# Streaming encoder layer on one core: the gate of p by seven half products a pair, and the end by halves of the tokens

## Chip, core and metric

One core of one Trainium2 chip runs the kernel. The metric is the device time of one execution in microseconds (us), less being better. Three executions of the kernel before took 1573.99, 1574.2 and 1575.36 us; the median is 1574.2.

## What is computed

One layer of a hybrid encoder on 1024 prompt frames and 32 new frames, in fp32, D_MODEL = 1024. The part that matters here is the second half of the layer and its end:

```python
x = x + merged @ w_out
ffn_out, new_conv = conv_ffn(rmsnorm(x, g_ffn), conv_buf, w_up, w_dw, b_dw, w_down)
x = x + ffn_out
x = x + (p_i @ w_ple) * jax.nn.sigmoid(rmsnorm(x, g_ple) @ w_ple_gate)
...
y_prompt = rmsnorm(xp, g_final)
```

conv_ffn multiplies by w_up (1024 x 5632), convolves one half of the result over three frames, applies GELU, multiplies by the other half, and multiplies by w_down (2816 x 1024). Ahead of it lie an RMS norm, an input projection, pooling, banded attention of 8 heads and two gated projections.

## The kernel before

The tokens lie along the columns: T = 1056 = 1024 + 32, in three chunks of CW = 352 or in two halves of HT = 528. The channels lie on the 128 partitions, in KT = 8 tiles. Every fp32 product is made of three matmuls on a high and a low part of each factor (high x high, high x low, low x high). ACT rounds to the high part, DVE (for tokens) and POOL (for weights) subtract it to get the low part. The five engines run side by side; each instruction list is written out by hand and runs in order, and semaphores join them.

Weights come from w_stream. SP loads them in order; in the feed-forward a frame's tiles come in four halves (half_raw(0) to half_raw(3), 128 x 512). A load waits with half_free until POOL has made the low part of the piece that lay there. POOL's and ACT's pieces go through a ring of four places: piece q waits until PE is done with piece q - 4 (piece_event). pieces_upto on ACT makes the high parts up to a count, ahead of need.

The feed-forward is a list of frames. An up frame U (n = 0 to 21) makes two tiles of w_up, one of each half, with seven products of half size in the place of eight (Strassen's way in Winograd's form): seven weight pieces, of which some are sums of halves, against seven token operands op_hi/op_lo 0 to 6, each of HK = 4 tiles of HT columns. A frame has 7 x 4 x 3 x 2 = 168 matmuls of 264 columns (L952). A down group D (0 to 10) adds two rows of tiles to the residual x_res: UNITS = 24 units (8 tiles x 3 chunks), each of 6 matmuls of 352 columns (L976 to L978), in 8 banks; DVE adds each unit to x_res (down_add, L1829). The order is U0 U1 U2 D0 U3 U4 D1 ... U20 U21 D9 D10.

Behind D10 stands the end. p's product (K = 256, product(), L703) fills ple; the norm of x is summed on PE (norm, L741), rooted on ACT, inverted on DVE (invert_rms). The gate of p is eight tiles of 8 x 9 = 72 matmuls of 352 columns (L703), each read by DVE (scaled), passed through the sigmoid on ACT, multiplied by ple and added to x_res. Then the last norm, one reciprocal of 1056 columns, eight products by g_final (L1940) and eight stores. p itself is loaded by SP into p_raw, which shares its place with operands 5 and 6, so it has to wait until the last up frame's products are done:

```python
sp.wait_ge(ffn_done, UP[FT - 1].event + PRODUCTS)
sp.dma_start(p_raw[:], pT).then_inc(p_loaded, 16)
sp.wait_ge(piece_split, PIECES)
```

This stands behind the loop over all frames. At the start of the feed-forward the five operands 0 to 4 are made while w_out's product runs; operands 5 and 6 and the three sums of the norm (norm2, L960) come between the first frame's products, and root2 and invert2 make the reciprocals by thirds.

## Time and profile before

| what | us |
|---|---|
| median of three executions | 1574.2 |
| the profiled execution's own time | 1574.24 |
| its span | 1572.5 |
| busy: PE, DVE, POOL, ACT | 1517.8, 852.7, 676.3, 496.5 |
| mean granted TensorE clock | 0.989 of full speed |

The span runs from the first to the last instruction on the core; the rest of the execution's time lies around it. Engine names: PE is TensorE, DVE VectorE, ACT ScalarE, POOL GpSimd, SP SyncE, which here only issues DMAs. Matmuls overlap in the pipeline, so a matmul's own length is longer than its pitch, and the pitch is what counts. A granted clock of 1.00 is 2.4 GHz and 0.50 is 1.2 GHz. "Idle before" names what released an engine.

### The profile page before, as it was taken

Reading aid. Unit: us, or ns where it says so; the run is one execution under the profiler, and the core shown is the slowest. Engines: PE = TensorE matmul, PEld = TensorE weight load, DVE = VectorE, ACT = ScalarE, POOL = GpSimd, SP = SyncE. Lnnn points to the kernel's source line nnn. Section 1 sums busy time; section 2 is a strip of 40 time slices with the busy share of each in tenths; the row PEclk is TensorE's granted clock in tenths of the full one; section 3 lists DMA queues with packets and bytes.
Section 4 is the critical chain, followed back from the end, with each engine's and each line's share of the span. In section 5 each row is a group of like instructions: output and inputs, shape, how many; then the busy total and the mean of one; then the engine's idle time right before and its main releaser. Section 6 shows DMA issues by size and latency. Waiting matters only on the chain.

```text
span 1572.5 us, 25547 instructions
## 1 busy us (share of the span) xinstructions
PE 1517.8 (97%) x10616; PEld 1474.2 (94%) x10616; DVE 852.7 (54%) x1305; ACT 496.5 (32%) x875; POOL 676.3 (43%) x436
## 2 busy tenths in 40 slices
PE   7999999999999999998999999999999999999992
PEld 7988888889999999998999999999999999999992
DVE  7564444442231136668746547456474574687665
ACT  6025444443100021244432423323233233432211
POOL 2431213223343434345664655746556466623330
PEclk9999999999999999999999999999999999999996
DMA  6410212100111114111111201112012110311102
GB/s 239 138 43 15 71 58 69 35 27 28 41 54 41 41 54 151 41 33 49 55 37 52 74 28 54 55 43 66 28 55 63 46 55 28 99 52 41 41 14 110
DMA packets 37402, 91.33 MB, mean 58 GB/s; under 512 B 5528, under 2 KB 5536, under 8 KB 37160
## 3 DMA queue, kind: packets, MB, share of 16 engines
q1 hardware_dynamic: 34552, 80.95, 15.8%
q10 hardware_dynamic: 2736, 8.76, 1.4%
q8 instruction: 84, 1.38, 0.4%
q14 instruction: 30, 0.25, 0.0%
HBM read 83.00 MB, written 9.83 MB: 59 GB/s over the span
## 4 chain that ended last, share of the span: by engine, by line
PE 89%; DVE 5%; issue 2%; DMA 1%; ACT 1%; SPq 0%; POOL 0%; DVEq 0%; ACTq 0%; POOLq 0%
PE ps L703 28%; PE ps L952 27%; PE ps L976 5%; PE ps L978 5%; PE ps L977 5%; PE ps L715 4%; PE ps L717 4%; PE ps L716 4%; PE ps L838 2%; PE ps L860 2%; PE ps L812 2%; DVE h_lo L1369 1%; DMA x_in<-xT 1%; DVE acc L1429 1%; DVE x_res L1940 1%
## 5 line engine op out<-in xcount | busy, mean ns | idle before, releaser
L623 POOL TENSOR_TENSOR w_hi<-w_raw,zero 128x1024 fp32r<-128x1024 f32 x56 | 106.0, 1892 | 542.5 <-PE ps L703 252.2
L657 POOL TENSOR_TENSOR w_lo<-w_raw,w_hi 128x512 fp32r<-128x512 f32 x154 | 221.5, 1445 | 215.2 <-ACT w_hi L1198 215.2
L952 PE MATMUL ps<-op_hi,w_hi 128*128 128x264 f32 x1232 | 252.9, 286 | 3.7 <-DVE op_lo L1696 2.2
L952 PE MATMUL ps<-op_lo,w_hi 128*128 128x264 f32 x1232 | 252.2, 286 | 0.0
L952 PE MATMUL ps<-op_hi,w_lo 128*128 128x264 f32 x1232 | 251.8, 286 | 0.0
L952 PEld LDWEIGHTS ps<-op_hi,w_hi 128*128 128x128 f32 x1232 | 193.1, 189 | 5.3 <-DVE op_lo L1696 2.4
L952 PEld LDWEIGHTS ps<-op_lo,w_hi 128*128 128x128 f32 x1232 | 192.1, 189 | 0.0
L952 PEld LDWEIGHTS ps<-op_hi,w_lo 128*128 128x128 f32 x1232 | 191.8, 189 | 0.0
L715 PE MATMUL ps<-h_hi,w_hi 128*128 128x352 f32 x480 | 160.9, 335 | 10.5 <-DVE w_lo L1411 8.9
L976 PE MATMUL ps<-mid_hi,w_hi 128*128 128x352 f32 x528 | 170.2, 322 | 0.0
L977 PE MATMUL ps<-mid_lo,w_hi 128*128 128x352 f32 x528 | 170.0, 322 | 0.0
L978 PE MATMUL ps<-mid_hi,w_lo 128*128 128x352 f32 x528 | 170.0, 322 | 0.0
L1829 DVE TENSOR_TENSOR x_res<-ps,x_res 128x352 f32<-128x352 f32 x264 | 130.0, 520 | 52.0 <-PE ps L978 52.0
L717 PE MATMUL ps<-h_hi,w_lo 128*128 128x352 f32 x480 | 156.0, 325 | 0.0
L716 PE MATMUL ps<-h_lo,w_hi 128*128 128x352 f32 x480 | 155.7, 324 | 0.0
L1198 ACT ACTIVATE w_hi<-w_raw 128x512 fp32r<-128x512 f32 x154 | 97.2, 632 | 182.1 <-PE ps L952 98.6
L625 POOL TENSOR_TENSOR w_lo<-w_raw,w_hi 128x1024 fp32r<-128x1024 f32 x56 | 148.5, 2652 | 4.4
L703 PE MATMUL ps<-h_hi,w_hi 128*128 128x352 f32 x480 | 104.3, 325 | 3.7 <-DVE gap L1383 1.5
L703 PE MATMUL ps<-h_hi,w_lo 128*128 128x352 f32 x480 | 103.4, 323 | 0.0
L703 PE MATMUL ps<-h_lo,w_hi 128*128 128x352 f32 x480 | 103.3, 323 | 0.0
L715 PEld LDWEIGHTS ps<-h_hi,w_hi 128*128 128x128 f32 x480 | 91.7, 191 | 11.6 <-issue 8.9
L978 PEld LDWEIGHTS ps<-mid_hi,w_lo 128*128 128x128 f32 x528 | 99.4, 188 | 0.0
(207 smaller groups left out, 2768.6 us busy)
## 6 DMA issues: line engine op xcount, KB each, us to landing
w_raw<-w_stream SPq DMA_DIRECT2D x132, 256.0 KB, 2.8
w_raw<-w_stream SPq DMA_DIRECT2D x58, 512.0 KB, 3.7
x_in<-xT SPq DMA_DIRECT2D x8, 528.0 KB, 8.6
x_res<-xT ACTq DMA_DIRECT2D x8, 528.0 KB, 6.8
o_y<-x_res ACTq DMA_DIRECT2D x8, 528.0 KB, 2.9
bias_lines<-bias_line SPq DMA_DIRECT2D x1, 3072.0 KB
bias_sb<-bias_lines SPq DMA_DIRECT2D x4, 640.0 KB, 5.8
o_v<-vT SPq DMA_DIRECT2D x4, 272.0 KB, 2.1
```

The source lines that it names most:

```text
L623: pool.tensor_tensor(w_hi[k][:], w_raw[k][:], zero[:].broadcast_to([P, KT * P]), ALU.add).then_inc(w_hi_done, 1)
L625: pool.tensor_tensor(w_lo[k][:], w_raw[k][:], w_hi[k][:].bitcast(F32), ALU.subtract).then_inc(w_split, 1)
L657: pool.tensor_tensor(piece_lo(q), x, piece_hi(q).bitcast(F32), ALU.subtract).then_inc(piece_split, 1)
L703: mm = pe.matmul(out[:, c, :], w, x[:, c * CW:(c + 1) * CW], start=first and n == 0, stop=last and n == 2)
L715: pe.matmul(out, w_hi[k][:, col], x_h, start=b == 0, stop=False)
L716: pe.matmul(out, w_hi[k][:, col], x_l, start=False, stop=False)
L717: mm = pe.matmul(out, w_lo[k][:, col], x_h, start=False, stop=b == KT - 1)
L952: mm = pe.matmul(region(fr, i, c), w[:, col], x[i][:, b, c * HW:(c + 1) * HW], start=opens and b == 0 and n == 0, stop=b == HK - 1 and n == 2,
L976: pe.matmul(out, piece_hi(q)[:, col], x_h, start=b == 0, stop=False)
L977: pe.matmul(out, piece_hi(q)[:, col], x_l, start=False, stop=False)
L978: mm = pe.matmul(out, piece_lo(q)[:, col], x_h, start=False, stop=b == 1)
L1829: dve.tensor_tensor(x, bank(fr.unit_bank(u), CW), x, ALU.add).then_inc(ffn_read, 1)
```

## The change

1. **Gate of p by half products.** Four frames H (n = 22 to 25) are put behind the feed-forward, two tiles of w_ple_gate each, with the same seven products as an up frame, in another order (ROLES, OPERANDS, PIECE_HALF). The operands 0 to 6 are now made of x after the feed-forward, scaled by g_ple. Four quarters of a pair (two tiles, two halves of the tokens: quarter) are read, scaled by the reciprocals, passed through the sigmoid, multiplied and added by turns. The copies out of the first three products go to tmp and a spare half row.
2. **Last down group and p's product as one frame Z.** MIXED lists the 24 units of D10 and behind them 24 units of p's product, in the same eight banks. DVE adds two units at once (down_pair, 704 columns). ACT copies p's units two at once to ple (ple_out). Between these, DVE (first_ops, second_ops), ACT (tile_ops) and POOL (base_out, x times g into p_raw's place) make operands 0 to 4 as each tile is finished, and the sum of squares.
3. **p is loaded behind the loads of U21**, ahead of those of D9, since Z and H need loads of their own.
4. **End by halves of the tokens.** The last norm is summed, rooted, inverted and multiplied for the right half and then for the left; 16 stores of 264 KB go from SP and ACT by turns.
5. **Roots ahead at the start of the feed-forward.** The third sum of the norm goes behind product 5 of the first frame; on ACT the first two roots stand ahead of the high parts of operand 6, the third behind them.

The core of the diff:

```diff
+FREES = {"U": (2, 0, 1, 3), "H": (1, 0, 2, 3), "D": (2, 0, 1, 3), "Z": (2, 0, 1, 3)}
-FRAMES += [("U", FT - 2), ("U", FT - 1), ("D", GROUPS - 2), ("D", GROUPS - 1)]
+FRAMES += [("U", FT - 2), ("U", FT - 1), ("D", GROUPS - 2), ("Z", GROUPS - 1)]
+FRAMES += [("H", FT + _r) for _r in range(KT // 2)]
+MIXED = [("D", _u) for _u in range(UNITS)] + [("E", _u) for _u in range(UNITS)]
...
@@ sync: loads @@
+                if fr is UP[FT - 1]:
+                    sp.wait_ge(ffn_done, fr.event + PRODUCTS)
+                    sp.dma_start(p_raw[:], pT).then_inc(p_loaded, 16)
+            for i in range(0, 2 * KT, 2):
+                sp.wait_ge(y_ready, i + 1)
+                cols = slice(HT, T) if i < KT else slice(0, HT)
+                sp.dma_start(o_y[i % KT][:, cols], x_res[:, i % KT, cols]).then_inc(stored, 16)
...
@@ gpsimd @@
+            def base_out(i):
+                pool.wait_ge(ffn_read, tile_read(i))
+                pool.wait_ge(p_split, 2)
+                pool.tensor_tensor(base_row(i), x_res[:, i, 0:HT],
+                                   g_sb[:, 2 * KT + i:2 * KT + i + 1].broadcast_to([P, HT]), ALU.mult).then_inc(y_made, 1)
+                    for i in range(fr.pieces):
+                        if i in (4, 6):
+                            base_out(i - 4)
+                            base_out(i - 3)
+                        piece_low(fr.piece + i, half_raw(HALVES[i % 4]))
...
@@ tensor @@
+            def mixed():
+                for s, (kind, u) in enumerate(MIXED):
+                    if s % 6 == 0:
+                        pe.wait_ge(piece_split, q + 1)
+                    if s < 8:
+                        pe.wait_ge(ffn_read, fr.read + s - 7)
+                    elif MIXED[s - 8][0] == "D":
+                        pe.wait_ge(ffn_read, fr.read + MIXED[s - 8][1] // 2 + 1)
+                    else:
+                        pe.wait_ge(ple_read, MIXED[s - 8][1] // 2 + 1)
...
             up(0, 4, ready=(5, 5))
-            pe.wait_ge(root_done, 4)
-            norm2(2, bank(0, CW))
             up(0, 5, ready=(21, 1))
+            pe.wait_ge(root_done, CH + 1)
+            norm(2, 2, bank(0, CW))
             up(0, 6, ready=(25, 1))
...
@@ scalar @@
+            def tile_ops(m):
+                act.wait_ge(ffn_read, tile_read(m))
+                i = m % HK
+                if m < HK:
+                    op_high(0, i, x_res[:, m, 0:HT], m, 0, gain=2)
+                    square(x_res[:, m, :], 2 * KT + m)
+                    op_high(1, i, None, None, 20 + i + 1)
+                else:
+                    op_high(3, i, x_res[:, m, 0:HT], m, 0, gain=2)
+                    op_high(2, i, None, None, 24 + 2 * i + 1)
+                    square(x_res[:, m, :], 2 * KT + m)
+                    op_high(4, i, None, None, 24 + 2 * i + 2)
...
+            def copy_h(r, name, i):
+                act.wait_ge(ffn_done, fr.event + i + 1)
+                if r > 0:
+                    act.wait_ge(h_added, 4 * (r - 1) + 2 + i)
...
@@ vector @@
+            def down_pair(r):
+                dve.wait_ge(ffn_done, LAST.event + MIXED.index(("D", 2 * r)) + 2)
+                dve.tensor_tensor(x, out, x, ALU.add).then_inc(ffn_read, 1)
...
+            dve.wait_ge(h_added, 2 * KT)
+            for n, half in ((1, slice(HT, T)), (2, slice(0, HT))):
+                invert(3 * CH + n, half)
+                dve.wait_ge(rms_ready, 3 * CH + n)
+                for k in range(KT):
+                    dve.scalar_tensor_tensor(out=x_res[:, k, half], in0=x_res[:, k, half], scalar=g_col(3, k),
+                                             in1=rms[:, half], op0=ALU.mult, op1=ALU.mult).then_inc(y_ready, 1)
```

First listing: SP's list around the load of p, before. The 128x512 loads are halves of down tiles, the last of them those of D10.

```order
L606 DMA w_raw0_49<-w_stream 128x512 [waits piece_split]
L606 DMA w_raw1_50<-w_stream 128x512 [waits piece_split]
L608 DMA p_raw_113<-pT 128x2112 [waits ffn_done]
L540 DMA w_raw1_50<-w_stream 128x1024 [waits w_split,piece_split]
L540 DMA w_raw0_49<-w_stream 128x1024 [waits w_split]
```

And now; the two halves ahead of p are the last of U21, the two behind it the first of D9.

```order
L641 DMA w_raw0_50<-w_stream 128x512 [waits piece_split]
L641 DMA w_raw1_51<-w_stream 128x512 [waits piece_split]
L660 DMA p_raw_113<-pT 128x2112 [waits ffn_done]
L641 DMA w_raw0_50<-w_stream 128x512 [waits piece_split]
L641 DMA w_raw1_51<-w_stream 128x512 [waits piece_split]
```

The load of p, with its wait for U21's last product, moved from behind D10's four loads to ahead of D9's; 28 loads of halves now follow it.

Second listing: DVE's list at the last down group, before. x_res<-ps is the add of a unit, h_lo the low part of a tile of the gate's input.

```order
L1820 TENSOR_TENSOR mid_lo_108<-b_row_110,mid_hi_104 128x1056 [waits mid_hi_done,mid_ready]
L1829 TENSOR_TENSOR x_res<-ps,x_res 128x352 [waits ffn_done] x12
L1864 TENSOR_TENSOR p_lo<-p_raw,p_hi 128x1056 [waits p_hi_done] x2
L1829 TENSOR_TENSOR x_res<-ps,x_res 128x352 [waits ffn_done] x10
L1369 SCALAR_TENSOR_TENSOR h_lo<-x_res,g_sb,h_hi 128x1056 [waits hi_done,ffn_read]
```

And now, around the twelfth and last pair of the group (the x_res row near the end):

```order
L2033 TENSOR_TENSOR x_res<-ps,x_res 128x704 [waits ffn_done] x2
L1592 TENSOR_TENSOR acc<-acc,tmp 128x1056 [waits acc_done,sq_done]
L1883 SCALAR_TENSOR_TENSOR op_sum_88<-x_res,g_sb,op_sum_85 128x528 [waits ffn_read]
L1881 TENSOR_TENSOR op_sum_94<-op_sum_88,p_raw 128x528 [waits op_sum]
L1891 TENSOR_TENSOR op_lo_84<-op_sum_85,op_hi_83 128x528 [waits op_hi_done]
L1893 SCALAR_TENSOR_TENSOR op_lo_90<-x_res,g_sb,op_hi_89 128x528 [waits op_hi_done]
L1891 TENSOR_TENSOR op_lo_87<-op_sum_88,op_hi_86 128x528 [waits op_hi_done,op_sum]
L1891 TENSOR_TENSOR op_lo_93<-op_sum_94,op_hi_92 128x528 [waits op_hi_done]
L2033 TENSOR_TENSOR x_res<-ps,x_res 128x704 [waits ffn_done]
```

A sum of squares and six operand instructions stand ahead of the last read of the group's banks.

Third listing: ACT's list where p's first two units are copied out of their banks (ple<-ps). The four rows ahead of it are tile 5's; tile 4's four stand ahead of these. Before, DVE read p's product and ACT had only the high parts and squares here.

```order
L1297 ACTIVATE op_hi_89<-x_res,g_sb 128x528 [waits ffn_read]
L1295 ACTIVATE op_hi_86<-op_sum_88 128x528 [waits op_sum]
L1128 ACTIVATE tmp<-x_res 128x1056 [waits acc_done]
L1295 ACTIVATE op_hi_92<-op_sum_94 128x528 [waits op_sum]
L1438 ACTIVATE ple<-ps 128x704 [waits ffn_done]
L1288 ACTIVATE w_hi_52<-w_raw_51 128x512 [waits ffn_done,half_loaded3]
```

Each of the four waits for DVE, and the copy that frees two banks of PE comes behind them.

## Rows read from the trace of the kernel before

**Rows 1.** Page, part 4: shares of the chain by engine.

```profile
PE 89%; DVE 5%; issue 2%; DMA 1%; ACT 1%; SPq 0%; POOL 0%; DVEq 0%; ACTq 0%; POOLq 0%
```

**Rows 2.** Windows of PE by stage: window, length, busy (instructions), granted clock, DMA share, GB/s.

```profile
1393.10:1416.30 23.20, 23.03 (x144) 1.00 0.22 70
1416.30:1441.70 25.40, 23.85 (x144) 1.00 0.12 42
1441.70:1458.10 16.40, 13.62 (x78) 1.00 0.11 33
1458.10:1539.90 81.80, 81.77 (x504) 1.00 0.08 27
1539.90:1572.50 32.60, 3.49 (x6) 0.61 0.33 133
```

**Rows 3.** Chain of waits, last up frames: start, length, what.

```profile
1339.95 29.98 PE ps L952 x245
```

**Rows 4.** Timeline of PE, start of the feed-forward; in brackets idle time before.

```profile
717.96 1.54 PE L960 MATMUL ps<-acc,ones 128*128 128x352 f32 x2 [3.78 <-ACT rms L1261]
...
727.45 0.64 PE L952 MATMUL ps<-op_hi,w_hi 128*128 128x264 f32 x2 [2.17 <-DVE op_lo L1696]
...
736.18 0.48 PE L952 MATMUL ps<-op_hi,w_hi 128*128 128x264 f32 x2 [0.33 <-ACT b_row L1238]
```

**Rows 5.** Windows of PE: granted clock behind two idle stretches.

```profile
718.00:721.00 3.00, 3.00 (x11) 0.53 0.00 0
...
1545.00:1548.00 3.00, 0.66 (x1) 0.50 0.00 0
```

**Rows 6.** Timelines of DVE and ACT, second up frame.

```profile
732.83 1.22 DVE L1784 TENSOR_TENSOR a_row<-a_row,rms 128x1024 f32<-128x1024 f32 x1
...
735.45 0.59 ACT L1238 ACTIVATE b_row<-ps 128x528 f32<-128x528 f32 x1
```

**Rows 7.** DMA issues, w_raw's tile view, SP's timeline.

```profile
w_raw<-w_stream SPq DMA_DIRECT2D x132, 256.0 KB, 2.8
...
p_raw<-pT SPq DMA_DIRECT2D x1, 1056.0 KB, 6.8
...
L606 SPq DMA_DIRECT2D w_raw<-w_stream x16: 327/328/328, 1310.4 to 1372.1; - x16
...
1372.46 0.43 SPq L608 DMA_DIRECT2D p_raw<-pT  x1
```

**Rows 8.** Groups by line of ACT, 690 to 745 us.

```profile
L1205 ACT ACTIVATE op_hi<-op_sum 128x528 fp32r<-128x528 f32 x6 | 3.8, 642 | 10.9 <-DVE op_sum L1686 10.9
...
L1261 ACT ACT_TABLE_LOAD x1 | 1.3, 1283 | 0.0
...
L1238 ACT ACTIVATE b_row<-ps 128x528 f32<-128x528 f32 x2 | 1.2, 592 | 0.0
```

**Rows 9.** Timelines of DVE and POOL, last up frames and groups.

```profile
1348.99 1.80 DVE L1789 TENSOR_TENSOR b_row<-b_row,rms 128x528 f32<-128x528 f32 x1
...
1370.20 0.70 DVE L1789 TENSOR_TENSOR b_row<-b_row,rms 128x528 f32<-128x528 f32 x1
...
1404.36 0.95 DVE L1829 TENSOR_TENSOR x_res<-ps,x_res 128x352 f32<-128x352 f32 x2
...
1350.19 1.76 POOL L677 TENSOR_TENSOR w_raw<-w_raw,w_sum 128x512 f32<-128x512 f32 x1
...
1388.07 1.30 POOL L657 TENSOR_TENSOR w_lo<-w_raw,w_hi 128x512 fp32r<-128x512 f32 x1 [4.48 <-ACT w_hi L1198]
```

**Rows 10.** Chain of waits behind the last gate matmul.

```profile
1544.91 1.09 ACT tmp L1028
...
1546.02 1.26 DVE acc L1378
...
1552.05 6.75 DVE rms L1384
...
1561.37 7.38 DVE x_res L1940 x6
```

More of the change, by code:

```diff
@@ L141 @@
 FRAME, PIECES, EVENTS, READS = frames_of_ffn()
-UP = {f.n: f for f in FRAME if f.kind == "U"}
-DOWN = {f.n: f for f in FRAME if f.kind == "D"}
+UP = {f.n: f for f in FRAME if f.kind in "UH"}
+DOWN = {f.n: f for f in FRAME if f.kind in "DZ"}
+LAST = DOWN[GROUPS - 1]
 def piece_event(q):
@@ L733, in tile_ready @@
                 pe.wait_ge(w_split, s + 1)
-            def norm(n, evac, ready):
-                pe.wait_ge(acc_done, ready)
-                pe.wait_ge(evacuated, evac)
-                out = job_set(n)
-                for c in range(CH):
-                    mm = pe.matmul(out[:, c, :], ones[:], acc[:, c * CW:(c + 1) * CW], start=True, stop=True)
-                mm.then_inc(norm_done, 1)
             pe.wait_ge(consts_made, n_consts)
@@ L1007, in _, with last_norm @@
-            for m in range(KT):
-                tile_ready(S_PGATE + m)
-                product((J_PGATE + m, J_PGATE + m - 1), 1 - m % 2, h2_hi, h2_lo,
-                        ready=(h_split, KT + 1) if m == 0 else None).then_inc(tile_done, 1)
-                if m == 0:
-                    norm(J_NORM3, J_NORM3 - 1, 3 * (KT - 1))
-            norm(J_NORM4, J_NORM4 - 1, 4 * (KT - 1))
+            def last_norm(name, out, terms):
+                half = 0 if name == "L" else HT
+                for c in range(2):
+                    for n, x in enumerate(terms):
+                        mm = pe.matmul(out[:, c * 512:c * 512 + HW], ones[:], x[:, half + c * HW:half + (c + 1) * HW],
+                                       start=n == 0, stop=n == len(terms) - 1)
+                mm.then_inc(norm_done, 1)
@@ new lines, in _ @@
+            ple_out(2)
+            pieces_upto(first + 1)
+            ple_out(3)
+            tile_ops(7)
+            ple_out(4)
+            ple_out(5)
+            pieces_upto(first + 2)
+            for i in range(HK):
+                op_high(5, i, x_res[:, HK + i, HT:T], HK + i, 0, gain=2)
+                ple_out(6 + i)
+            pieces_upto(first + 3)
+            ple_out(10)
+            ple_out(11)
+            def copy_h(r, name, i):
+                fr = UP[FT + r]
+                act.wait_ge(ffn_done, fr.event + i + 1)
+                if r > 0:
+                    act.wait_ge(h_added, 4 * (r - 1) + 2 + i)
+                elif i == 1:
+                    act.wait_ge(pool_stored, 32)
+                else:
+                    act.wait_ge(acc_done, 3 * (KT - 1))
+                act.activation(halves(quarter(r, name)[2]), product_out(fr, i), ACT.Copy).then_inc(ffn_copied, 1)
@@ new lines, in last_root @@
+            def last_root(name, n, out):
+                half = slice(0, HT) if name == "L" else slice(HT, T)
+                act.wait_ge(norm_done, 3 * CH + n)
+                act.activation(halves(rms[:, half]), out.rearrange("p (c n) -> p c n", c=2)[:, :, 0:HW], ACT.Sqrt,
+                               bias=eps[:], scale=1.0 / D_MODEL).then_inc(root_done, 1)
+            r = KT // 2 - 1
+            sigmoid_h(r, "bL")
+            square_h(r, "aL")
+            last_root("R", 1, ps[:, 6 * 512:8 * 512])
```

567 lines of the change are left out of this document (386 added, 181 removed).

## The prediction

> **What bounds the kernel now.** I read the shares of the chain first: PE has 89% of it [rows 1], so a change counts by what it takes from PE's stream or by what makes PE wait. Then PE by stages [rows 2]: it has next to no gap in the last down group (23.2 us), loses 1.5 us around p's product, 2.8 us around the norm behind the first gate tile, nothing in the other seven, and from 1539.9 to 1572.5 it does three small sums: 32.6 us of tail. The pitch prices matmuls: 29.98/245 = 0.122 us for 264 columns in the chain [rows 3], and 23.2/144 = 0.161 us for 352 in the unbroken group [rows 2]. Last, the start of the feed-forward: PE waits 3.8 us for a root and 2.2 us for a low half, [rows 4], and behind the first its clock is at 0.53 for 3.0 us [rows 5], so 1.4 us more go.
>
> The sum is made against the profiled execution: span 1572.5, its own time 1574.24, 1.7 us around it; the median of the three runs is 1574.2, so nothing is to be added.
>
> **1. Start of the feed-forward: 0 (-2 to +1).** Product 5 of the first frame moves ahead of the third norm, so the 3.8 us wait goes from there. But PE waits again at 727.4 for the last low half and is held at 736.18 by a copy that ACT makes only behind the first convolution; that waits for DVE's scaling of a_row, which ends at 734.05 [rows 6] behind three reciprocals of a third each. DVE worked nearly without a break from 712.4 to there, in the same order as in the change. The earlier product only makes PE's second wait longer. What is late next is this queue of DVE. Were both waits to go, and 1.4 us of low clock behind each, it would be 3.8 + 2.2 + 2.8 = 8.8 us: a rival.
>
> **2. Down group 9 (DOWN[9]): +10 (+5.4 to +12).** The load of p has to wait until the last up frame's seventh product is done. Before, it stood behind all loads of down halves. Now it stands ahead of them (first order listing), and those of group 9 need it to be issued, though their places are free long before. U21 ends at 1369.9. p would be issued at 1370.05, the first half 0.45 later. Before, the last half at 1372.1 and p at 1372.46 moved together and the later one landed at 1372.46 + 6.8 = 1379.3, 7.2 us behind the first issue; alone a half takes 2.8 us [rows 7]. So it lands between 1370.5 + 2.8 = 1373.3 and 1370.05 + 7.2 = 1377.25; then ACT's high half 0.64 [rows 8], POOL's low half 1.30 [rows 9] and handovers 0.1: PE starts between 1375.3 and 1379.3, a hole of 5.4 to 9.4 us where there was none. I take 8.5, near the upper end, since p's bytes are ahead of the half's. After so long a hole the clock is at 0.50 to 0.53 for some 3 us [rows 5]: 1.5 us more. ACT's convolution for the last row is queued behind these pieces, but its result is needed 23 us later. The Trainium skill (DMA: Bandwidth & Descriptors, section on queues, rings and completion order) says that descriptors are consumed in ring order and that a semaphore's increment lands only after the engine's earlier writes; by that alone the half would come at the upper end and the hole would be 9.4. No row here shows two queued transfers apart.
>
> **3. Last down group and p's product (frame Z): +8.4 (+3.8 to +13).** Its matmuls are the same 288, 48 units of 6: 288 x 0.161 = 46.5 us against 48.6 before (1393.1 to 1441.7). But DVE and ACT now also make five operands of half products beside them, and PE's banks wait on these queues. Zero is the group's start. DVE: a read of two banks takes 0.85 (x2 of 352: 0.95, less one start), an op of 528 columns 0.70, of which 0.63 stay back to back, and 0.8 before one that needs it [rows 9], a sum of squares 1.25 [rows 10]. Behind the fourth pair (8.6) DVE has until the twelfth: 8 reads 6.8, four times two ops 5.6, 3 sums 3.75, six ops of the second kind 4.0: 20.2, so 28.8. PE's unit 30 waits for this twelfth read at 29.0, so this is no wait by itself. But a DVE op with both inputs in SBUF that meets a running POOL op takes 1.1 us longer (1.80 against 0.70 for the same op) [rows 9]. POOL's four products by g and its low halves meet three or four of these: 32.5, a wait of 3.5. Then ACT. Its first copy out of p's banks stands behind the sixth tile's operands (third listing): DVE's sum 1.25 and first op 0.8 give 34.6, ACT's high half 0.64, square 1.07, high half 0.64, copy 0.7 (0.59 for 528 columns) [rows 8]: 37.5, where unit 32 wants it at 34.4: 3.1. DVE goes on with 5 ops 3.2, a sum 1.25 and 1.1 for a meeting, one op 0.8: 40.9; ACT the same four again: 43.8, where unit 34 wants it at 39.5: 4.3, and with it low clock: 1.5. In all 46.5 + 3.5 + 3.1 + 4.3 + 1.5 = 58.9. Without any meeting or low clock the same steps give 52.4. I take 57, nearer the upper one as both effects have their rows: 57 - 48.6 = +8.4.
>
> **4. Gate of p (frames H): -8.5 (-13 to -3).** 576 matmuls of 352 (1441.7 to 1539.9 = 98.2 us with the norm) become 4 x 168 = 672 of 264: 672 x 0.122 = 82.2, three norm sums (their six records took 3.49 at mostly half clock [rows 2, 5], so some 1.95 at full), a wait of 0.3 for a read before the seventh product: 84.5. Against 98.2 that is -13.7. What comes back, counted from the group's end: ACT has operand 6's last high half at 15.5, behind a copy and two pieces that wait for product 3 (13.7). DVE: low half, reciprocal of a third (6.75/3 = 2.25), low half: 18.5; two reads 19.8; two reciprocals 24.3; scale, sigmoid (0.65), product and sum of quarter one 27.0; scale of quarter two, read and scale of quarter three 29.0; product and sum of quarter two 30.4, and 0 to 2 more for meetings with POOL. Only this frees the buffer into which ACT copies (square ahead of it, 0.6 each) product 0 of the second frame: 31.6 to 33.6, where PE wants it at 28.7. So 2.9 to 4.9 there, and 1 to 1.5 in the later frames: 5.2. 84.5 + 5.2 = 89.7, so -8.5. Weight pieces are no new wait: POOL makes 11 ops per 20.55 us in an up frame and PE runs through two of them unbroken [rows 3].
>
> **5. Tail: -8.3 (-10 to -6).** Before 32.6: four ops of 1.27 or 1.09, square, sum, norm and root until 1552.05, reciprocal 6.75, eight products of 1.23, last store 3.7 [rows 10]. Now behind the last matmul only one quarter is open: read 0.7, sigmoid 0.65, product and sum 1.35: 2.8. The right half's root is later: sigmoid, square 0.6, table 1.28, root 0.6 on ACT: 3.9. Then DVE: reciprocal 3.4, eight products 5.05, reciprocal 3.4, eight products 5.05, store 3.5: 3.9 + 16.9 + 3.5 = 24.3. The left half's norm (six sums of 264, root) is done by 11, and the right half's 8.45 us, which run until 12.35, hide it.
>
> **Sum:** 0 + 10 + 8.4 - 8.5 - 8.3 = +1.6: 1574.24 + 1.6 = 1575.8, rounded **1576**. What is gained (2.1 of small gaps around p's product, 13.7 at the gate, 8.3 in the tail: 24.1) is given back as new waits (10 + 10.5 + 5.2 = 25.7). Its own range, with the terms' doubts against each other, is 1571 to 1581. A difference of 0.2% (3.1 us) is what a measurement can tell here.
>
> **Rivals.**
> - *Side engines keep up* (0.17): few meetings of DVE and POOL. Group 3 ends at 52.4 (-4.6), the gate gives back 2.5 instead of 5.2, the hole is 7.5: -8.3 from the sum, 1567.5. For it: DVE has gaps in which POOL can work; against it: the op of [rows 9] is hit in each up frame that follows another.
> - *DVE bounds the half products, slower* (0.13): in a gate frame DVE has 4 reads and 15 ops from SBUF, 4 x 0.7 + 15 x 0.65 = 12.6 us, and POOL 11 ops. Each meeting costs 1.1, so from (20.55 - 12.6)/1.1 = 7.2 meetings of 11 the frame is longer than PE's; with all eleven it is 24.7, +4.1 in three frames less the 1 counted: +11, 1587. Against it: an up frame has the same eleven POOL ops and about as many of DVE, and PE runs through two of them unbroken [rows 3]. The Trainium skill (SBUF: State Buffer, section on its two separate sides) calls the shared pair of ports an exclusive lock under which the loser fully blocks; the 1.1 us of [rows 9] agree with it, near the 1.3 of a POOL op, and by that rule alone all eleven would be met.
> - *The half overtakes p* (0.08): hole 5.4, clock cost 0.7: 1572.
> - *The start gives its idle time back* (0.07): the 8.8 us of part 1, 1567. Against it: DVE's queue there is unchanged.
> - *Something else is late* (0.03): 1585.
> - The forecast has 0.52: 0.04 below 1571, 0.26 within 0.2%, 0.22 above.
>
> Faster 0.04 + 0.17 + 0.04 + 0.07 = 0.32; same 0.26 + 0.04 = 0.30; slower 0.22 + 0.13 + 0.03 = 0.38. The range that leaves two in ten out reaches into both outer cases: 1566 to 1585.
>
> **What would show it.** PE idle for 5 to 9 us between the last product of 264 columns and the first matmul of down group 9, released by POOL's low half behind a DMA; three waits of 3 to 5 us in the 12 units around the 30th to 36th of the last group, on a DVE read and on ACT's copies of p's banks; one wait of 3 to 5 us in the second gate frame; PE's first matmul behind the third product of the second up frame still near 736; from the last matmul to the end 24 us. It is wrong if PE runs from 1369.9 without a hole, or if the last group with p's product takes under 50 us, or if a gate frame takes over 22.

## The result: 1586.4 us, slower by 0.8%

The changed kernel takes 1586.44 us (median of four runs, 1585.56 to 1588.31) against 1574.1 for the kernel before beside it (1572.73 to 1575.36): ratio 1.008, interval 1.0063 to 1.0098, so 12 us slower. The forecast was 1576 with a range to 1585; the time lies 1.4 us outside it, on the side of the rival "DVE bounds the half products".

The stages of the changed kernel, read against [rows 2]: window, length, busy us (instructions) of PE, PEld, DVE, ACT and POOL, then clock, DMA share and GB/s. The five rows are the hole after the last up frame, down group 9 and the last of its kind, frame Z, the four gate frames up to their last product, and the tail.

```profile
1372.30:1380.30 8.00, 0.01 (x1) 0.01 (x1) 0.71 (x1) 1.89 (x4) 1.35 (x2) 0.64 0.76 266
1380.30:1405.60 25.30, 25.28 (x144) 25.30 (x145) 18.19 (x30) 7.87 (x12) 8.51 (x6) 0.91 0.23 75
1405.60:1463.40 57.80, 49.94 (x291) 48.93 (x290) 51.79 (x56) 34.43 (x51) 22.51 (x16) 0.94 0.07 24
1463.40:1556.80 93.40, 86.79 (x679) 84.94 (x677) 82.31 (x81) 44.08 (x75) 57.25 (x38) 0.98 0.11 35
1556.80:1584.30 27.50, 7.46 (x21) 5.31 (x20) 22.02 (x24) 5.07 (x8) 0.00 (x0) 0.66 0.41 158
```

PE's granted clock is the last figure but two; DVE is busy for 82.3 of 93.4 us in the gate frames. PE's waits in them and around them, by the timeline of PE of the changed kernel (start, duration, in brackets idle time before and its releaser):

```profile
722.70 0.78 PE L1007 MATMUL ps<-op_hi,w_hi 128*128 128x264 f32 x2 [7.43 <-DVE b_row L1964]
...
736.62 0.48 PE L1007 MATMUL ps<-op_hi,w_hi 128*128 128x264 f32 x2 [1.85 <-ACT b_row L1328]
...
1380.32 0.63 PE L1031 MATMUL ps<-mid_hi,w_hi 128*128 128x352 f32 x1 [8.01 <-issue]
...
1437.57 0.40 PE L1059 MATMUL ps<-p_hi,w_hi 128*128 128x352 f32 x1 [2.67 <-DVE x_res L2033]
...
1442.14 0.43 PE L1059 MATMUL ps<-p_hi,w_hi 128*128 128x352 f32 x1 [2.41 <-ACT ple L1438]
...
1448.29 0.43 PE L1059 MATMUL ps<-p_hi,w_hi 128*128 128x352 f32 x1 [2.78 <-ACT ple L1438]
...
1484.78 0.48 PE L1007 MATMUL ps<-op_hi,w_hi 128*128 128x264 f32 x2 [1.90 <-issue]
...
1496.72 0.48 PE L1007 MATMUL ps<-op_hi,w_hi 128*128 128x264 f32 x2 [2.90 <-ACT spare_half L1496]
...
1525.43 0.49 PE L1007 MATMUL ps<-op_hi,w_hi 128*128 128x264 f32 x2 [0.57 <-ACT tmp L1496]
...
1547.92 0.48 PE L1007 MATMUL ps<-op_hi,w_hi 128*128 128x264 f32 x2 [0.70 <-ACT tmp L1496]
```

The terms against the prediction, in us against the profile of before. The first is counted from the end of w_out's product to the third product of the second up frame. That end came 2.4 us earlier than before; why, no run told (in the other runs it came from 0.1 us later to 3.1 us earlier; in the two that were made from the kernel before, 0.1 later and 1.7 earlier).

| Part | forecast | measured |
|---|---|---|
| start of the feed-forward | 0 | +2.9 |
| up and down frames, to the end of U21 | 0 | +1.9 |
| down group 9 | +10 | +10.1 |
| frame Z | +8.4 | +9.2 |
| gate frames | -8.5 | -4.8 |
| tail | -8.3 | -5.1 |
| before the feed-forward | 0 | -2.4 |
| sum | +1.6 | +11.8 (spans 1572.5 and 1584.3) |

Group 9 and frame Z came as forecast. Four parts did not: two that were costed at nothing, and the two gains.

The gate frames one by one, from the first matmul of each to that of the next. "Forecast" is the prediction's part 4 shared out by frame, "short POOL" the run further down in which POOL has next to nothing to do here:

| us | frame 1 | frame 2 | frame 3 | frame 4 |
|---|---|---|---|---|
| forecast | 22.8 | 24.4 | 21.2 | 21.2 |
| changed kernel | 24.4 | 25.2 | 21.4 | 22.5 |
| short POOL | 22.8 | 23.8 | 20.6 | 20.6 |

The products alone take 168 x 0.122 = 20.5 us a frame. What is above the forecast is explained for the most part by DVE and POOL side by side. Timelines of the changed kernel at the end of DVE's work on the second gate frame and its reads of product 6 (L2180) in all four, then POOL:

```profile
1497.63 0.69 DVE L2180 TENSOR_TENSOR tmp<-ps,rms 128x528 f32<-128x528 f32 x1
...
1511.63 1.78 DVE L2200 TENSOR_TENSOR tmp<-tmp,ple 128x528 f32<-128x528 f32 x1
1513.44 1.69 DVE L2202 TENSOR_TENSOR x_res<-x_res,tmp 128x528 f32<-128x528 f32 x1
1515.05 1.79 DVE L2200 TENSOR_TENSOR spare_half<-spare_half,ple 128x528 f32<-128x528 f32 x1
...
1518.49 0.69 DVE L2180 TENSOR_TENSOR tmp<-ps,rms 128x528 f32<-128x528 f32 x1
...
1540.99 0.70 DVE L2180 TENSOR_TENSOR tmp<-ps,rms 128x528 f32<-128x528 f32 x1
...
1559.60 0.70 DVE L2180 TENSOR_TENSOR tmp<-ps,rms 128x528 f32<-128x528 f32 x1
...
1511.09 1.75 POOL L728 TENSOR_TENSOR w_sum<-w_sum,w_raw 128x512 f32<-128x512 f32 x1
1512.92 1.64 POOL L710 TENSOR_TENSOR w_lo<-w_sum,w_hi 128x512 fp32r<-128x512 f32 x1
1514.53 1.75 POOL L733 TENSOR_TENSOR w_raw<-w_raw,w_sum 128x512 f32<-128x512 f32 x1
```

The two engines go in lockstep: each DVE operation from SBUF starts about half a microsecond behind a POOL operation's start and ends about as far behind its end, 1.7 us instead of 0.7, and POOL's take 1.65 to 1.75 instead of 1.3 [rows 9]. The reads of product 6 lie 20.86, 22.50 and 18.61 us apart: only the middle one is clearly longer than PE's 20.5, and the last is shorter, as DVE had fallen behind and catches up. The expectations below take 22.5 for each of the frames 2 to 4, which is not so. In the middle stretch DVE is busy for 20.97 us and PE for 21.66 (windows, columns as above):

```profile
1518.50:1541.00 22.50, 21.66 (x175) 21.29 (x175) 20.97 (x21) 10.07 (x18) 16.93 (x12) 1.00 0.16 48
```

### The profile page after: what moved, and what is told of

Same layout as the page of the kernel before. It is cut to its first block, busy times and chain, and to the rows that moved or that the text cites. A ratio compares the mean times of both kernels' runs of the same rounds, so it can differ in the third digit from the quotient of the medians.

```text
span 1584.3 us, 26063 instructions
## 1 busy us (share of the span) xinstructions
PE 1516.3 (96%) x10726; PEld 1471.0 (93%) x10726; DVE 892.5 (56%) x1374; ACT 537.6 (34%) x970; POOL 708.9 (45%) x468
## 4 chain that ended last, share of the span: by engine, by line
PE 85%; DVE 8%; issue 3%; ACT 2%; DMA 1%; POOL 1%; SPq 0%; DVEq 0%; ACTq 0%; POOLq 0%
PE ps L1007 29%; PE ps L766 21%; PE ps L1031 5%; PE ps L1032 5%; PE ps L1033 5%; PE ps L778 4%; PE ps L780 4%; PE ps L779 4%; PE ps L891 2%; PE ps L913 2%; PE ps L865 2%; DVE rms L2038 1%; DVE x_res L2268 1%; DVE tmp L2200 1%; DVE op_sum L1883 1%
## 5 line engine op out<-in xcount | busy, mean ns | idle before, releaser
L1007 PE MATMUL ps<-op_hi,w_hi 128*128 128x264 f32 x1456 | 299.4, 287 | 18.4 <-DVE b_row L1964 7.4
L1007 PE MATMUL ps<-op_lo,w_hi 128*128 128x264 f32 x1456 | 298.1, 286 | 0.0
L1007 PE MATMUL ps<-op_hi,w_lo 128*128 128x264 f32 x1456 | 297.9, 286 | 0.0
L778 PE MATMUL ps<-h_hi,w_hi 128*128 128x352 f32 x480 | 159.4, 332 | 10.4 <-DVE w_lo L1606 9.3
L779 PE MATMUL ps<-h_lo,w_hi 128*128 128x352 f32 x480 | 155.5, 324 | 0.0
L780 PE MATMUL ps<-h_hi,w_lo 128*128 128x352 f32 x480 | 155.4, 324 | 0.0
L778 PEld LDWEIGHTS ps<-h_hi,w_hi 128*128 128x128 f32 x480 | 90.7, 189 | 11.8 <-issue 9.2
L1031 PEld LDWEIGHTS ps<-mid_hi,w_hi 128*128 128x128 f32 x480 | 91.2, 190 | 8.2 <-issue 8.2
L710 POOL TENSOR_TENSOR w_lo<-w_sum,w_hi 128x512 fp32r<-128x512 f32 x52 | 91.6, 1762 | 10.3 <-ACT w_hi L1288 6.4
L779 PEld LDWEIGHTS ps<-h_lo,w_hi 128*128 128x128 f32 x480 | 90.8, 189 | 0.2
L1032 PEld LDWEIGHTS ps<-mid_lo,w_hi 128*128 128x128 f32 x480 | 90.9, 189 | 0.0
```

Of the source, the lines that this page charges most:

```text
L710: pool.tensor_tensor(piece_lo(q), x, piece_hi(q).bitcast(F32), ALU.subtract).then_inc(piece_split, 1)
L778: pe.matmul(out, w_hi[k][:, col], x_h, start=b == 0, stop=False)
L779: pe.matmul(out, w_hi[k][:, col], x_l, start=False, stop=False)
L780: mm = pe.matmul(out, w_lo[k][:, col], x_h, start=False, stop=b == KT - 1)
L1007: mm = pe.matmul(region(fr, i, c), w[:, col], part[x][:, b, c * HW:(c + 1) * HW], start=opens and b == 0 and n == 0, stop=b == HK - 1 and ...
L1031: pe.matmul(out, piece_hi(q)[:, col], x_h, start=b == 0, stop=False)
```

## Experiments

Every run is compared with the kernel before on its own chip; the changed kernel stands at 1.008. A ratio's interval reaches 0.001 to 0.002 to each side, 1.5 to 3 us, so that parts of 1 or 2 us are read from the stages of the traces, not from the medians alone.

### p's load behind group 9's halves

```
-                if fr is UP[FT - 1]:
-                    sp.wait_ge(ffn_done, fr.event + PRODUCTS)
+                if fr is DOWN[GROUPS - 2]:
+                    sp.wait_ge(ffn_done, fr.before.event + PRODUCTS)
                     sp.dma_start(p_raw[:], pT).then_inc(p_loaded, 16)
```

> The changed kernel with p's load moved behind the four loads of down group 9 (it still waits for the last up frame's seventh product). Theory 1 (the load of p stands ahead of loads that were ready long before): the halves of group 9 are on the chip when U21 ends, PE's idle time of 8.0 us ahead of it goes, and the stretch of half clock behind it: 8 to 10 us less, about 1577. Rival (the side engines' pieces are what is late, or the new last group waits for p instead): the hole only moves into group 9 or to p's first unit, and the time falls by less than 3 us.

1578.37 us, ratio 1.0021 (1.0012 to 1.0031): 8 to 9 us less. Windows of this run, the last up frame and group 9 (columns as above):

```profile
1352.00:1375.40 23.40, 23.40 (x193) 23.40 (x192) 16.56 (x21) 10.17 (x19) 18.30 (x11) 1.00 0.15 46
1375.40:1398.70 23.30, 23.30 (x147) 23.30 (x146) 19.81 (x33) 7.87 (x12) 6.20 (x4) 1.00 0.38 128
```

PE goes from one into the other at full clock. The hole and group 9 take about 10 us less than in the changed kernel (8.0 of waiting and 2.1 of low clock behind it), and the frames behind it are as long as in the changed kernel (Z and gate 57.7 and 93.5). Theory 1 holds; the order of one queue was 8 us of the 12 by the medians.

### The first frame's order of before

PE's third norm goes back ahead of product 5, and on ACT:

```
-            pieces_upto(8)
-            root(1, 0, bank(0, CW))
-            root(1, 1, bank(1, CW))
+            pieces_upto(7)
             op_high(6, 0, None, None, 12 + 2)
             op_high(6, 1, None, None, 12 + 4)
-            pieces_upto(9)
+            root(1, 0, bank(0, CW))
+            root(1, 1, bank(1, CW))
+            pieces_upto(8)
```

> The changed kernel with the first frame's order of before: PE's third norm ahead of product 5, ACT's roots behind the first two late operands. Theory 1 (the roots ahead delay the pieces behind them, so POOL's sums fall among DVE's late sums): 2 to 3 us less, about 1583.5, and PE's first matmul behind product 2 of the second up frame comes 40 to 41 us after the first m_hi unit of w_out's end instead of 43.8. Rival (the 2.9 us come from where buffers lie or from the run): within 0.7 us of the changed kernel.

1583.31 us, ratio 1.0054 (1.004 to 1.0068): 3 to 4 us less; theory 1 said 2 to 3, and by the stages it is 2.9 in the start. The reverse, the kernel before with the roots ahead alone:

> The kernel before with one part of the change alone, the roots ahead: PE's product 5 of the first frame ahead of the third norm, ACT's eighth weight piece and first two roots ahead of the first late operands, and the third root behind piece 10. Theory 1 (the part costs what undoing it gave back): 2.5 to 4 us more than before, about 1578, with POOL's sums between 710 and 720 us making four of DVE's late sums 1.7 to 1.8 us long. Rival (the cost came only together with the shift of the buffers or the rest of the change): within 1 us of before.

1576.42 us, ratio 1.0008 (1.0000 to 1.0017): 1.3 us more, 0 to 2.7, less than theory 1 said and not cleanly apart from the rival. The traces agree better. From the first product of the feed-forward to the third product of the second up frame PE takes 39.75 to 40.2 us in the seven kernels that have the old order, and 42.5 to 42.7 in the ten that have the roots ahead. The second late sum and the first low half of operand 6 on DVE's timeline, with the roots ahead (first fence, kernel before with this part) and in the old order (second, changed kernel without it):

```profile
714.01 1.79 DVE L1688 SCALAR_TENSOR_TENSOR op_sum<-x_res,g_sb,op_hi 128x528 f32<-128x528 f32 x1
715.83 1.68 DVE L1686 TENSOR_TENSOR op_sum<-op_sum,op_lo 128x528 f32<-128x528 f32 x1
717.43 1.77 DVE L1696 TENSOR_TENSOR op_lo<-op_sum,op_hi 128x528 fp32r<-128x528 f32 x1
```

```profile
712.05 0.76 DVE L1883 SCALAR_TENSOR_TENSOR op_sum<-x_res,g_sb,op_hi 128x528 f32<-128x528 f32 x1
712.85 0.71 DVE L1881 TENSOR_TENSOR op_sum<-op_sum,op_lo 128x528 f32<-128x528 f32 x1
713.47 0.70 DVE L1891 TENSOR_TENSOR op_lo<-op_sum,op_hi 128x528 fp32r<-128x528 f32 x1
```

From the first late sum to the end of the scaling of a_row DVE needs 24.3 us with the roots ahead (712.59 to 736.93; 24.5 in the changed kernel) and 21.6 without (710.62 to 732.21). ACT's eighth weight piece now comes ahead of its waits for DVE, so POOL begins its six operations for the frame while DVE makes its sums, 5.6 us sooner (at 713.4 instead of 719.0 in the kernel before, whose feed-forward starts within 0.2 us of this one). Five of DVE's operations of 528 columns take over 1.3 us then instead of three, and DVE is busy for 2.8 us more in the stretch.

### The place of the weight buffers

The kernel before with u_tail and the gap ahead of w_raw, and the changed kernel with w_raw where it was (half a buffer over constants and u_tail that are no longer used):

```
+        u_tail = fixed("u_tail", [2 * PAIRS, HIST])
+        cursor[0] += 1120
         w_raw = [fixed(f"w_raw{k}", [KT * P]) for k in range(2)]
```

> The kernel before with one change: u_tail and a gap of 1120 bytes stand ahead of the weight buffers, as in the changed kernel, so that w_raw, w_hi, w_lo and all behind them lie 2112 bytes further on; no instruction differs. Theory 1 (the place of the weight buffers sets a small part of the matmuls' pitch): the frames from the second up frame to the last take 635.6 us instead of 633.8, as in the changed kernel, and the time is 0 to 2 us above that of before. Rival (placement does nothing, the 1.9 us are the chip's or the run's): the frames stay at 633.8 and the time within 1 us of before.

> The changed kernel with the weight buffers where they were before: the half buffer that the gate needs lies over gate_b, pool_sc, dw, conv_hist, conv_new, inv_cnt and u_tail, which stand last, instead of over u_tail and a gap ahead of w_raw (ACT's first copy into it also waits for the store of conv_new; it shifted them by 1600 bytes, not by the 2112 that was written for the run before_place). Theory 1 (the 1.9 us in the frames of the feed-forward are the place of the buffers): the matmuls of 352 columns in the down groups are back from a median of 324 to 322 ns, and the time is 1.5 to 2.5 us less, about 1584.3. Rival: no change.

1576.50 us, ratio 1.0014 (1.0005 to 1.0023), and 1585.04 us, ratio 1.0062 (1.0048 to 1.0076): 2.3 us more and 1.4 less by the medians. One line of a matmul of the down groups (count, then minimum, median and maximum in ns), of the kernel before, of it with the shift, of the changed kernel, and of that with the old place:

```profile
L976 PE MATMUL ps<-mid_hi,w_hi x432: 320/322/328, 771.5 to 1307.6; 128*128 128x352 f32 x144
```

```profile
L977 PE MATMUL ps<-mid_hi,w_hi x432: 318/324/330, 771.7 to 1309.7; 128*128 128x352 f32 x144
```

```profile
L1031 PE MATMUL ps<-mid_hi,w_hi x432: 318/324/330, 771.9 to 1310.0; 128*128 128x352 f32 x144
```

```profile
L1031 PE MATMUL ps<-mid_hi,w_hi x432: 320/322/328, 773.3 to 1309.5; 128*128 128x352 f32 x144
```

From the fourth product of the second up frame to the start of U21's last pair of matmuls it is 630.35 us before, 632.23 with the shift, 632.27 in the changed kernel, and with the old place 630.35 again. All seventeen traces fall into these two groups: 630.2 to 630.4 in the six with the old place, 632.1 to 632.3 in the eleven with the new. Shifting the weights by 1600 bytes costs 1.9 us over the feed-forward, with not one instruction changed; 0.20 us of it come in each of the nine down groups, 1.8 in all. Theory 1 holds for this stage; why the place does it is open. The matmuls of 264 columns show no such step in their median (285 ns in both).

### What fills the gate frames

> The changed kernel with POOL's eleven operations of the gate frames 2 to 4 made on 8 columns instead of 512, and pieces 1 and 2 copied from a loaded half (it leaves out most of the low halves and the sums of weights in these frames; PE, ACT and DVE have the same operations). Theory 1 (DVE's operations meet POOL's and take 1.7 to 1.8 us instead of 0.7, and DVE's queue sets the gate frames): no DVE operation of these frames over 1.1 us, the frames 20.5 to 21 us instead of 22.5, the time 4 to 6 us less, about 1581. Rival (the order of DVE's steps and the handovers to ACT set the frames, whatever an operation takes): less than 2 us.

1580.56 us, ratio 1.0039 (1.0025 to 1.0053): 6 us less. DVE's timeline of this run shows the same steps at 0.7, and the read of product 3 of two frames 20.55 us apart, each time behind 4 us of idle time:

```profile
1521.47 0.70 DVE L2190 TENSOR_TENSOR tmp<-tmp,ps 128x528 f32<-128x528 f32 x1 [3.99 <-PE ps L1012]
...
1528.71 0.71 DVE L2205 TENSOR_TENSOR spare_half<-spare_half,ple 128x528 f32<-128x528 f32 x1
...
1542.02 0.70 DVE L2190 TENSOR_TENSOR tmp<-tmp,ps 128x528 f32<-128x528 f32 x1 [3.99 <-PE ps L1012]
```

The four frames take 87.8 us instead of 93.4 and PE bounds the last two again. In the first its wait of 1.90 us ahead of product 6 falls to 0.32. In the second the wait for ACT's copy stays, at 2.94 (2.90 in the changed kernel), but the product behind it runs at full clock and takes 3.0 us, not 4.5; why the clock held this time no run tells. So the meetings with POOL cost 5.6 us in these frames, and the order of DVE's steps is not what sets the later two, while the one wait in the second frame is left to it. The next run asks the same from the other side:

```
                 read_h(r, "bL")
+                add_h(r, "bL")
                 if not last:
                     acc_h(r, "aR")
                     acc_h(r, "bR")
-                add_h(r, "bL")
-                if not last:
```

> The changed kernel with DVE's sums of squares of quarters one and two behind the product and sum of quarter four in the first three gate frames. Theory 1 (DVE's chain sets the frames and holds ACT's copy of product 2, so these sums and their waits for ACT's square, 1.9 us a frame between the read of product 6 and the product by the gate, are on the path): 3 to 5 us less, about 1582. Rival (the meetings with POOL alone set the frame, the sums take the same time wherever they stand): within 1.5 us.

1589.64 us, ratio 1.0096 (1.008 to 1.0112): slower by 3 us, against both theories: one wait of 3.87 us ahead of product 6 of the third frame. The four sums of squares, which took two by two 1.99 and 1.52 us in the changed kernel, now stand in one row beside POOL's low halves:

```profile
1522.19 6.95 DVE L2214 TENSOR_TENSOR acc<-acc,ple 128x528 f32<-128x528 f32 x4
```

What an operation of DVE costs depends on where POOL is: a sum between two POOL operations costs 0.75, a sum beside one 1.74. Taking them away altogether:

> The changed kernel without DVE's eleven sums of squares in the gate frames: PE's last two norms add up all eight squares themselves (16 matmuls of 264 columns each instead of 4 and 6). Theory 1 (DVE's queue, lengthened by meetings with POOL, sets the gate frames; each sum costs it 0.7 to 1.8 us): frames 2 to 4 fall from 22.5 us to 20.6 to 21, the last norms are hidden behind ACT's table load and DVE's reciprocal, and the time is 4 to 7 us less, about 1581. Rival (the longer norms come out in the tail, or other operations meet POOL instead): within 2 us of the changed kernel.

1586.45 us, ratio 1.0077 (1.0063 to 1.0091): no gain. In the stages the gate frames fell to 91.7, less than was expected, and the tail rose to 28.8: each norm took 7.1 us, not the 2 that I had counted on, since a matmul of 264 float32 columns with ones takes 0.446 us against 0.122 for the rounded operands. A miss of the design. Shared between the two engines:

> The changed kernel with DVE keeping only the five sums of squares of the right half of the first three gate frames, behind the product and sum of quarter four; PE's last norms take the rest (three terms for the right half, eight for the left, a term of 264 columns costing 0.446 us in each of two banks by the run that gave PE all of them). Theory 1 (DVE's length bounds gate frames 2 to 4, and PE is free in the tail until ACT's table is loaded, and for the left half until DVE has made the right half's outputs): the frames gain what they gained with all sums on PE, about 4 us, and the tail gives back less than 1: 3 to 4.5 us less, about 1582.5. Rival (a sum left to DVE meets POOL and costs 1.7 us wherever it stands, five of them 8.5 us, as when they were only moved): within 1 us of the changed kernel.

1586.03 us, ratio 1.0074 (1.006 to 1.0087): by the medians nothing, by the stages -2.7 in the gate frames (90.7, the last two 20.6 each) and +0.9 in the tail, where theory 1 had 3 to 4.5 less in all. In the tail the left half's norm came too late (timeline of PE, ACT and DVE of this run):

```profile
1561.16 0.71 PE L1104 MATMUL ps<-acc,ones 128*128 128x264 f32 x2 [4.01 <-ACT ple L1515]
1561.68 4.96 PE L1104 MATMUL ps<-ple,ones 128*128 128x264 f32 x14
...
1570.25 0.70 ACT L1557 ACTIVATE rms<-ps,eps 128x528 f32<-128x528 f32 x1 [9.23 <-PE ps L1104]
...
1570.98 3.45 DVE L2038 RECIPROCAL rms<-rms 128x528 f32<-128x528 f32 x1 [1.38 <-ACT rms L1557]
```

### The order in Z and in the first gate frame

```
             down_pair(10)
+            down_pair(11)
             squares3(3)
             second_ops(0)
-            down_pair(11)
```

and on ACT ple_out(0) to ple_out(5) ahead of or inside tiles 4 to 7.

> The changed kernel with another order in the last down group: DVE reads the twelfth pair right behind the eleventh, and ACT copies p's banks out 0 to 5 ahead of or inside the operands of tiles 4 to 7 instead of behind them. Theory 1 (PE's three waits of 2.67, 2.41 and 2.78 us are the order of these queues): they go, and with them some of the stretch of half clock; the group with p's product takes 50 to 52 us instead of 57.8. What DVE has left to do then delays products 2 and 3 of the first gate frame, so the time falls by 3 to 7 us. Rival (DVE has no slack in this frame, so the waits move whole into the first gate frame): less than 2 us.

1584.00 us, ratio 1.0067 (1.0053 to 1.0081): 2 us less, between the two theories. The wait for the twelfth pair is gone, the frame takes 56.3 instead of 57.8 (theory 1 said 50 to 52), and two waits of 2.06 and 4.97 us stand in place of three: the copies 6 and 7 were now behind tile 7, whose sums DVE made beside POOL. One reciprocal earlier:

> The changed kernel with DVE's reciprocal of the first third of the root ahead of its low halves of operand 6 (where it stood idle for 2.6 us waiting for ACT) instead of behind the third of them. Theory 1 (the chain from the root to ACT's copy of product 0 of the second gate frame runs through this queue): PE's waits of 1.9 and 2.9 us shrink by 2.3 us together and the half clock behind them goes, 2 to 4 us less unless DVE's later frames take it back. Rival (frames 2 to 4 are bound by DVE anyway, and what it gains in frame 1 is carried through, or lost): exactly 2.3 or 0.

1585.76 us, ratio 1.0072 (1.0058 to 1.0085): 0.7 us less by the medians, which are too coarse for it. By the stages the gate frames take 91.0 us instead of 93.4, 2.2 of it in the first: the wait of 1.90 is gone, that of 2.90 stays at 2.92. That is theory 1. In the trace it is hidden by 2.3 us that come ahead of it and have nothing to do with the edit: 0.8 before the feed-forward, and 1.5 in the third product of the second up frame, which takes 4.5 us at low clock in six of the seventeen traces, of kernels with and without the change, and 3.0 in the others.

### Together

> The changed kernel with p's load behind group 9's halves, the first frame's order of before, the reciprocal of the first third early, sums of squares shared between DVE and PE as in acc_split, and the last down group with all of ACT's copies 0 to 7 of p's banks ahead of tile 7's second operand. Theory 1 (each part has its own stall): 8.6 + 3.6 + 0.7 + 3.5 + 3 to 5 us less than the changed kernel, 1565 to 1568, and 6 to 9 us less than the kernel before. Rival (the side engines' work in the last down group and the first gate frame is a sum that no order takes away, so that shorter waits there come back in the next stage): 1570 to 1573.

> best2 with the weight buffers where they were before, as in place_back. Theory 1: another 1.5 to 2.5 us less than best2, 1563 to 1566. Rival: as best2.

1571.69 us (ratio 0.9984, 0.9975 to 0.9993) and 1571.29 us (0.9984, 0.9975 to 0.9994). That is the rival's time, not theory 1's. In the second kernel the old place of the buffers gives its 1.9 us in the feed-forward again (630.35), and 0.4 by the medians, less than theory 1 said: in the two traces 1.1 us ahead of the feed-forward and 0.6 behind it stand against it. The first is 14.8 us less than the changed kernel, and the parts one by one had given 8.1 + 3.1 + 2.4 + 0.7 + 0.4 = 14.7 by their medians, but this agreement is chance. By the stages p's load and the first frame gave 13.2 us apart and give 13.2 together, while the other three gave 2.3 + 2.5 + 1.8 = 6.6 us in Z, gate frames and tail, and only 1.1 together. Z does fall, to 52.0 us in the second kernel (best3), but its gate frames rise to 96.9, for DVE is not ready with the first of them and PE waits 6.8 us there. Is that order or sum? The left norm early (first), and then DVE's reads of the first gate frame ahead of its late sums:

```
+            last_norm("L", ps[:, 4 * 512:6 * 512], (acc, *(ple[:, k, :] for k in range(1, KT - 2))), last=False)
             pe.wait_ge(ffn_read, READS)
             pe.wait_ge(h_sq, 2 * KT)
+            last_norm("L", ps[:, 4 * 512:6 * 512], (ple[:, KT - 2, :], ple[:, KT - 1, :]), first=False)
```

> best3 with six of the eight terms of the left half's last norm made by PE right behind the right half's norm, in the two banks that product 3 has left, and only two terms after the last square. Theory 1 (in acc_split PE's left norm of 9.1 us, part of it at half clock, ended 1.4 us behind the point where DVE wanted it): DVE runs from the right half's outputs into the left half's reciprocal without a wait, 1 to 2 us less than best3, 1569.3 to 1570.3. Rival (DVE wants it no earlier): 0.

> best4 with DVE reading products 3 and 4 of the first gate frame between its late sums, and all three reciprocals behind the last low half of operand 6. Theory 1 (the first gate frame is bound by the sum of DVE's work up to the fourth quarter; no order takes it away): PE's wait of 6.8 us ahead of product 6 falls by 4 to 5 us and comes back as a wait of 4 to 5 us ahead of the second gate frame; the time within 1 us of best4. Rival (the order matters: product 6 is on the path to everything behind it): 3 to 5 us less.

1570.36 us (ratio 0.9972, 0.9963 to 0.9981) and 1572.35 us (0.9985, 0.9976 to 0.9994). The first is the fastest kernel of this study, 4.4 us below the kernel before; DVE runs into the left reciprocal without a wait. In the second PE's wait moves, as theory 1 said, but it comes back larger, and the time is 2.0 us more than best4's, outside the 1 us that theory 1 allowed and the other way from the rival:

```profile
1469.59 0.51 PE L1007 MATMUL ps<-op_hi,w_hi 128*128 128x264 f32 x2 [1.70 <-DVE op_lo L1894]
...
1471.30 0.51 PE L1007 MATMUL ps<-op_hi,w_hi 128*128 128x264 f32 x2 [0.70 <-DVE op_lo L1894]
...
1485.48 0.78 PE L1007 MATMUL ps<-op_hi,w_hi 128*128 128x264 f32 x2 [7.31 <-ACT spare_half L1499]
```

The windows of the faster one say why; the first is the first gate frame with the start of the second, the other the 20.6 us behind it (columns as above):

```profile
1443.20:1484.50 41.30, 33.08 (x235) 32.08 (x236) 40.28 (x35) 19.27 (x31) 22.35 (x14) 0.88 0.09 26
1484.50:1505.10 20.60, 19.77 (x162) 19.59 (x161) 17.21 (x17) 10.16 (x18) 16.98 (x11) 1.00 0.16 52
```

DVE is busy for 40.3 of the first 41.3 us. That stretch is a sum of DVE's work; of the two orders that were tried neither shortens it, and no run took work out of it in this kernel.

## Why the prediction was wrong

- **1, start of the feed-forward: 0 forecast, +2.9.** The prediction said that DVE's queue sets the time there, "in the same order as in the change", and that was so. The step that failed is that the same order takes the same time: it looked at the order of DVE and not at what POOL does beside it, though the roots ahead move ACT's eighth piece, which releases POOL. The runs with and without the part show 24.3 and 21.6 us for the same DVE operations. PE's waits shifted as forecast: the 3.8 for the root went, and 7.43 came behind it. The forecast's sign for this part, a matmul "still near 736", came at 736.62 by luck, as all ahead of it was 2.4 us early.
- **The feed-forward between: 0, +1.9.** Not costed at all: the diff's line that moves u_tail was read as an allocation without a price. Two runs, one each way, show that it has one: 1.9 us.
- **2, down group 9: +10, +10.1.** Right in mechanism and size. The hole is 8.01 against 8.5 (and 9.4 at the upper end), the low clock behind it costs 2.1 against 1.5 (0.50 in the first 3 us), and one queue's order undone takes both away.
- **3, Z: +8.4, +9.2.** Right in the queues and in the total, 57.8 against 57, but the total is partly luck: the waits, on the releasers it named, are 2.67, 2.41 and 2.78 where the sum of 58.9 had 3.5, 3.1 and 4.3, which is 3.0 less, and the low clock costs 3.3 (57.7 less 46.5 of matmuls and 7.9 of waits) where it had 1.5. Its other reading, that these are the order of the queues, holds only in part: the better orders gave 1.5 and then 5.7 us in this frame, and DVE gave the second of these back behind it.
- **4, gate frames: -8.5, -4.8.** The products' own time was right (82.2 and three norm sums of 1.8 are 84.0; with short POOL operations the frames took 87.8, 3.3 of it waits). Three terms were too small, by 3.7 us together. The "wait of 0.3 for a read before the seventh product" is 1.90: DVE's low halves of operand 6 meet POOL, and with short POOL operations it is 0.32. The "2.9 to 4.9" in the second frame is 2.90, but 1.6 of low clock behind it stood in no term of part 4. The "1 to 1.5 in the later frames" is 2.9 in the last two, 1.8 of it waits. With it failed the step that spoke for unbroken later frames, that an up frame has as many operations and PE runs through it. The rival's threshold was 7.2 meetings of 11: in the middle stretch between reads DVE's longer operations add up to 8.3 us over 0.7 each, 7.5 meetings' worth, and 12.6 + 8.3 = 20.9 is just past PE's 20.5. On top DVE stood idle for 1.5 us, which the rule left out, 0.71 for ACT's sigmoid between two of its own steps and 0.37 for ACT's copy: 22.5. The stretches before and behind it have 5.1 and 2.8 us of such lengthening and take 20.9 and 18.6. So that rival had 0.13 and came in part, in one stretch of three. The Trainium skill (SBUF — State Buffer, section on its two separate sides) calls the shared ports an exclusive lock. That DVE and POOL take turns agrees with it; that by this rule alone all eleven operations would be met comes near in the middle stretch, where ten are lengthened and six of them fully, and in neither of the others.
- **5, tail: -8.3, -5.1.** Mis-sized by 3.2 us: 27.5 instead of 24.3. "Behind the last matmul only one quarter is open" was not so, two were: at PE's last product, 1556.8, DVE had only added up quarter three, with its scaling, a handover to ACT of 0.7 us, product and sum still to come, and read quarter four at 1559.6. The reciprocal starts 6.8 us behind the last product, not 3.9. What follows came near the forecast: 3.46 + 5.52 + 3.37 + 4.9 and 3.4 for the store.

Of the 10.2 us between forecast and trace, the two parts costed at nothing make 4.8, the gate frames 3.7, the tail 3.2 and the other two 0.9, less the 2.4 ahead of the feed-forward. The start and most of the gate frames have one cause, DVE's operations beside POOL's. Of the tail that explains 0.9 at most: with short POOL operations it was still 26.6, so the rest is DVE's own queue and its handovers; no run changed these alone. Of the prediction's signs of being wrong one came, a gate frame over 22 us. By its own terms the first two had to be over 22, so that only the fourth, with 22.5 us where 21.2 was forecast, says anything.

## What to carry to other kernels

Price an edit by what it releases on the other engines, not by the order of the engine that is waited for: here a weight piece that ACT made earlier set POOL to work 5.6 us sooner, beside DVE, and cost 2.9 us in a stage whose critical queue was unchanged. Where DVE and POOL both work from SBUF, count DVE's stage at the lengthened durations and with its handovers, and compare that sum with PE's before the products are made cheaper; past that point moving DVE's work only moved PE's wait here, so it is the work that should shrink. A load that may wait must stand behind the loads that are ready.

## What was not expected of the hardware

- DVE's operations with both inputs in SBUF and POOL's alternate in lockstep for as long as both have work: 1.68 to 1.80 us each on DVE (0.70 alone) and 1.64 to 1.75 on POOL (1.29 alone). Operations that read PSUM kept 0.69 to 0.71 in the same frames. POOL pays as well, by a third. One of each takes 1.7 us together, less than the 2.0 of the two alone added up.
- The place of the weight buffers in SBUF, 1600 bytes further on, lengthens the matmuls of 352 columns from 322 to 324 ns and the feed-forward by 1.9 of 630 us, in both directions and in all seventeen traces.
- A load of 1 MB ahead of four halves in one queue delayed the first of them to 5.5 us behind its issue (1372.72 to 1378.22) where one alone took 2.8 [rows 7]; p itself landed 5.1 us behind its own (1372.35 to 1377.44), 0.8 ahead of the half.
